# Gathering, turning and modulating all context rows once, in the router, instead of per expert

## The reference, cut to what matters

```
h    = modulate(rms_norm(y, norm_ffn), shift, scale)   # shift, scale differ for latent and context
aff  = softmax over tokens of (h @ w_router)           # 16 experts
g, idx = top_k(aff, cap)                               # each expert: 128 latent, 32 context tokens
xs   = h[idx]
ys   = (silu(xs @ w_gate) * (xs @ w_up)) @ w_down * g
y    = y + gate * scatter_add(ys, idx)
y_out = rms_norm(y, norm_final)
```

## Time and profile before

| what | us |
|---|---|
| median of 3 runs | 4124.34 (4119.36 to 4125.55) |
| span of the profiled execution | 4118.9 |
| PE / PEld / DVE / ACT / POOL busy | 3849.3 / 3382.8 / 2463.8 / 1832.2 / 503.2 |
| mean granted clock of PE, as a share of full speed | 0.968 |

### The profile page before, as it was taken

One profiled execution on the slowest core, in us unless ns is written; L12 is line 12 of the kernel. 1 busy time (PEld: TensorE's weight loads), 2 busy tenths in 40 slices (PEclk: granted clock), 3 DMA queues, 4 the chain that ended last, 5 costly groups with the idle time before them and its releaser, 6 DMA issues. The chain is left out here.

```text
span 4118.9 us, 68560 instructions
## 1 busy us (share of the span) xinstructions
PE 3849.3 (93%) x25046; PEld 3382.8 (82%) x25046; DVE 2463.8 (60%) x4732; ACT 1832.2 (44%) x2910; POOL 503.2 (12%) x501
## 2 busy tenths in 40 slices
PE   7899999999799999799997799999999999999992
PEld 3688888888688888799996688888888888888881
DVE  4645555555366666322325677777777777777774
ACT  3611111111267776211104566666666666666653
POOL 0000000000264653000000000000000000000000
PEclk9999999999899999899998799999999999999996
DMA  9434444444465553736316577778777777788876
GB/s 348 154 128 133 133 129 133 136 132 127 142 177 162 180 181 117 256 113 222 113 54 252 173 255 258 252 252 264 253 251 251 252 256 253 255 264 261 259 238 247
DMA packets 572379, 825.46 MB, mean 200 GB/s; under 512 B 23728, under 2 KB 458368, under 8 KB 560512
## 3 DMA queue, kind: packets, MB, share of 16 engines
q1 hardware_dynamic: 548448, 700.96, 52.1%
q0 software_dynamic: 23840, 123.26, 9.4%
HBM read 717.21 MB, written 108.00 MB: 200 GB/s over the span
## 5 line engine op out<-in xcount | busy, mean ns | idle before, releaser
L1977 DVE TENSOR_TENSOR e_wlo<-e_raw,e_whi 128x1024 fp32r<-128x1024 f32 x768 | 905.0, 1219 | 346.1 <-ACT e_whi L1897 342.9
L2109 PE MATMUL ps<-e_xs,e_whi 128*128 128x320 f32 x4096 | 1061.1, 345 | 13.9 <-DVE e_xs L1985 7.8
L2109 PE MATMUL ps<-e_xs,e_wlo 128*128 128x160 f32 x4096 | 935.3, 239 | 0.0
L1897 ACT ACTIVATE e_whi<-e_raw 128x1024 fp32r<-128x1024 f32 x768 | 768.6, 1054 | 321.2 <-DMA e_raw<-in_w_down 107.7
L2109 PEld LDWEIGHTS ps<-e_xs,e_whi 128*128 128x128 f32 x4096 | 755.2, 188 | 22.3 <-DVE e_wlo L1977 10.6
L2109 PEld LDWEIGHTS ps<-e_xs,e_wlo 128*128 128x128 f32 x4096 | 771.7, 191 | 0.7
L2127 PE MATMUL ps<-e_whi,e_h 128*128 128x512 f32 x1024 | 405.6, 396 | 8.5 <-DVE e_h L2011 8.5
L488 PE MATMUL ps<-hhi,p_whi 128*128 128x512 f32 (+1 forms) x1536 | 386.6, 360 | 8.5 <-DVE p_wlo L427 8.5
L445 DVE SCALAR_TENSOR_TENSOR p_acc<-p_modraw,cT,p_acc 128x256 f32<-128x256 f32 x960 | 386.4, 477 | 0.5 <-DMA p_modraw<-in_w_mod 0.5
L488 PE MATMUL ps<-hlo,p_whi 128*128 128x512 f32 (+1 forms) x1536 | 383.4, 358 | 0.0
L488 PE MATMUL ps<-hhi,p_wlo 128*128 128x512 f32 (+1 forms) x1536 | 383.1, 358 | 0.0
(11 more groups left out here) (245 smaller groups left out, 5498.7 us busy)
## 6 DMA issues: line engine op xcount, KB each, us to landing
e_raw<-in_w_gate SPq DMA_DIRECT2D x64, 2048.0 KB
e_raw<-in_w_up SPq DMA_DIRECT2D x64, 2048.0 KB
e_raw<-in_w_down SPq DMA_DIRECT2D x64, 2048.0 KB
p_modraw<-in_w_mod SPq DMA_DIRECT2D x128, 512.0 KB, 3.6
m_raw<-in_w_mod SPq DMA_DIRECT2D x16, 2048.0 KB, 14.6
p_raw<-in_w_in SPq DMA_DIRECT2D x64, 512.0 KB, 4.7
o_raw<-in_w_out SPq DMA_DIRECT2D x16, 2048.0 KB, 8.6
projT<-p_out_st POOLq DMA_DIRECT2D x32, 640.0 KB, 3.4
```

Of the source, the lines that this page charges most:

```text
L1897: nc.scalar.activation(piece(whi, c, q), piece(raw, c, q), ACT.Copy).then_inc(w_hi_made, 1)
L1977: nc.vector.tensor_tensor(piece(wlo, c, q), piece(raw, c, q), piece(whi, c, q).bitcast(F32), ALU.subtract).then_inc(w_lo_made, 1)
L2109: last = nc.tensor.matmul(bank[:, 0:cols], w[:, s, at:at + P], xs[:, k, 0:cols], start=(k == 0 and w is whi), stop=(k == KD - 1 and w is whi))
```

## The change

The context rows of all experts (16 x 32 = 512 rows) are gathered in four indirect DMAs of 128 rows (`idxG`, one column for each), into the first four tiles of `yt`, as soon as the fourth round of choosing is over. To have the 512 indices as four columns of 128, DVE spreads the 16 x 32 table by group (`numS`) and PE makes one small product with `group_of`. PE turns the four tiles (64 turns), ACT scales and shifts them (16 instructions of 512 columns) into a new tile `ctxT`, 128 x 16 x 512. The tables `gC` and `idxC` are turned and copied at the same place. In the instruction list of PE all this stands ahead of the turn of the latent tables.

In `experts`, POOL gathers only 128 latent rows, PE turns only these, in 4 groups of 4 blocks (two groups after each of the first two down chunks), ACT modulates only latent columns, and the context columns of `xs` are filled from `ctxT` by one ACT instruction (`ctx_high`) and one DVE instruction (`ctx_lo`) per expert, after the groups. To make room for `ctxT`, buffers are shared: gathered rows and `ys_l` are one tile `rows_l`, so `scale_ys` waits for the turns of the column blocks that it overwrites; `gact`, `hf` and `ctx_sum` go, their results written in place.

```diff
 # router, POOL
             pool.wait_ge(xn_stored, 16 * NT)
+            pool.wait_ge(ctx_step, 6)
+            for g in range(NCG):
+                nc.gpsimd.indirect_dma_start(yt[:, g, :], None, xn_d, bass.IndirectOffsetOnAxis(idxG[:, g:g + 1], 0)
+                                             ).then_inc(ctx_gathered, 16)
+            pool.wait_ge(ctx_gathered, 16 * NCG)
 # router, ACT
+            for k in range(KD):
+                act.wait_ge(ctx_turned, k + 1)
+                nc.scalar.activation(ctxT[:, k, :], ps[:, k % 4, :], ACT.Identity, bias=addT[:, 1, k:k + 1],
+                                     scale=mulT[:, 1, k:k + 1]).then_inc(ctx_modulated, 1)
 # router, PE
+            pe.wait_ge(ctx_step, 3)
+            for n, src in enumerate((topC, numC)):
+                nc.tensor.transpose(ps[0:CAP_C, 5, n * E:n * E + E], src[:], ident[0:E, 0:E]).then_inc(slots_turned, 1)
+            pe.wait_ge(ctx_step, 4)
+            nc.tensor.matmul(ps[:, 6, 0:NCG], numS[:].rearrange("e a s -> e (a s)"), group_of[:], start=True, stop=True
+                             ).then_inc(ctx_step, 1)
+            pe.wait_ge(ctx_gathered, 16 * NCG)
+            for k in range(KD):
+                if k < 4:
+                    pe.wait_ge(gate_read, 4 + k + 1)
+                else:
+                    pe.wait_ge(ctx_modulated, k - 3)
+                for g in range(NCG):
+                    last = nc.tensor.transpose(ps[:, k % 4, g * P:g * P + P], yt[:, g, k * P:k * P + P], ident[:])
+                last.then_inc(ctx_turned, 1)
+            for n, src in enumerate((topL, numL)):
+                pe.wait_ge(pick_step, PICKS + 7)
+                nc.tensor.transpose(ps[0:CAP_L, 7, n * E:n * E + E], src[:], ident[0:E, 0:E]).then_inc(slots_turned, 1)
 # router, DVE, in the rounds of choosing
+                if r == CAP_C // 8 - 1:
+                    nc.vector.tensor_copy(topC[:], top[64:64 + E, 0:CAP_C]).then_inc(ctx_step, 1)
+                    nc.vector.tensor_copy(numC[:], place[64:64 + E, 0:CAP_C]).then_inc(ctx_step, 1)
+                    ...
+                elif r == CAP_C // 8:
+                    dve.wait_ge(ctx_step, 5)
+                    nc.vector.tensor_copy(idxG[:], ps[:, 6, 0:NCG]).then_inc(ctx_step, 1)
+                    dve.wait_ge(slots_turned, 2)
+                    slots(CAP_C, 5, v["gC"], v["idxC"])
 # experts, ACT
+            def ctx_high(n):
+                act.wait_ge(xs_turned, n * NGR + NGR)
+                nc.scalar.activation(xs[:, :, CAP_L:CAP], ctxT[:, :, ds(n * CAP_C, CAP_C)], ACT.Copy).then_inc(xs_hi, 1)
 # experts, DVE
+            def ctx_lo(n):
+                dve.wait_ge(xs_hi, n * XSTEPS + XSTEPS)
+                nc.vector.tensor_tensor(xs[:, :, CAP + CAP_L:2 * CAP], ctxT[:, :, ds(n * CAP_C, CAP_C)],
+                                        xs[:, :, CAP_L:CAP].bitcast(F32), ALU.subtract).then_inc(xs_made, 1)
...
+                if not last:
+                    dve.wait_ge(xs_turned, e * NGR + (NGR + d + 1))
-                nc.vector.scalar_tensor_tensor(out=ys_l[:, cols], in0=ps[:, bank, :], scalar=aff_l[:, 0:1],
+                nc.vector.scalar_tensor_tensor(out=rows_l[:, cols], in0=ps[:, bank, :], scalar=aff_l[:, 0:1],
 # experts, PE, turn_xs
-                    for k in range(k0, k1):
-                        at = (k - k0) * CAP
-                        nc.tensor.transpose(ps[:, r % XB, at:at + CAP_L], xg_l[:, k * P:k * P + P], ident[:])
-                    for k in range(k0, k1):
-                        at = (k - k0) * CAP
-                        last = nc.tensor.transpose(ps[:, r % XB, at + CAP_L:at + CAP], xg_c[:, k * P:k * P + P],
-                                                   ident[0:CAP_C, 0:CAP_C])
+                    for i in range(KG):
+                        k = r * KG + i
+                        last = nc.tensor.transpose(ps[:, r, i * CAP_L:i * CAP_L + CAP_L], rows_l[:, k * P:k * P + P],
+                                                   ident[:])
```

More of the change, by code:

```diff
@@ L1547, in _ @@
                 act.wait_ge(y_turned, 4 * t + 4)
[L1548 removed]
+                nc.scalar.activation(yt[:, t, :], yt[:, t, :], ACT.Copy, scale=rinv[:, t:t + 1]).then_inc(y_scaled, 1)
             for c in range(2):
@@ new lines, in _ @@
+            dve.wait_ge(pick_step, PICKS)
+            nc.vector.tensor_copy(num[:], place[:]).then_inc(pick_step, 1)
+            nc.vector.tensor_copy(topB[:], top[32:32 + E, ::-1]).then_inc(pick_step, 1)
+            dve.wait_ge(pick_step, PICKS + 2)
+            nc.vector.tensor_scalar(numB[:], num[32:32 + E, ::-1], float(HALF), None, ALU.add).then_inc(pick_step, 1)
+            nc.vector.tensor_tensor(first[:], top[0:E, :], topB[:], ALU.is_ge).then_inc(pick_step, 1)
+            nc.vector.tensor_tensor(topL[:], top[0:E, :], topB[:], ALU.max)
@@ new lines, in _ @@
+            dve.wait_ge(pick_step, PICKS + 4)
+            nc.vector.tensor_tensor(numL[:], num[0:E, :], numB[:], ALU.subtract).then_inc(pick_step, 1)
+            dve.wait_ge(pick_step, PICKS + 5)
+            nc.vector.tensor_tensor(numL[:], numL[:], first[:], ALU.mult).then_inc(pick_step, 1)
+            dve.wait_ge(pick_step, PICKS + 6)
+            nc.vector.tensor_tensor(numL[:], numL[:], numB[:], ALU.add).then_inc(pick_step, 1)
+            dve.wait_ge(slots_turned, 4)
+            slots(CAP_L, 7, v["gL"], v["idxL"])
@@ L1765, in experts @@
     SLOTS = 2 * NP
-    NGR = 6
-    XB = 4
-    TURNS = (range(0, XB), range(XB, NGR))
-    GROUPS = [(3 * r, min(3 * r + 3, KD)) for r in range(NGR)]
+    NGR = 4
+    KG = KD // NGR
+    TURNS = (range(0, 2), range(2, NGR))
+    XSTEPS = NGR + 1
     index_set = sem("e_index_set")
@@ L1775, in experts @@
     xs_made = sem("e_xs_made")
-    gate_row, raw, w_loaded = (v[n] for n in ("gate_row", "raw", "w_loaded"))
+    gate_row, raw, w_loaded, ctxT = (v[n] for n in ("gate_row", "raw", "w_loaded", "ctxT"))
     w_hi_made = sem("e_w_hi_made")
@@ L1958, in expert @@
                         xs_high(e + 1, TURNS[c - NUP - 1])
+                        if c == NUP + 2:
+                            ctx_high(e + 1)
                 copy_ctx_low(e, ND - 1)
@@ L1964, in _ @@
                 xs_high(0, groups)
+            ctx_high(0)
             with act.Fori(0, E - 1) as e:
@@ L2049, in expert @@
                     else:
-                        scale_ys(e, c - NUP - 1)
+                        scale_ys(e, c - NUP - 1, last)
                     if following:
@@ L2061, in expert @@
                         build_xs(e + 1, TURNS[c - NUP - 1])
-                scale_ys(e, ND - 1)
+                        if c == NUP + 2:
+                            ctx_lo(e + 1)
+                scale_ys(e, ND - 1, last)
             make_lo(0, 0, range(NP))
             build_xs(0, range(NGR))
+            ctx_lo(0)
             with dve.Fori(0, E - 1) as e:
```

145 lines of the change are left out of this document (63 added, 82 removed).

## The result

The changed kernel takes 4055.31 us, median of 4 runs (4046.81 to 4061.72), against 4122.81 for the kernel before on the same chip: ratio 0.9835, 95% interval 0.9821 to 0.9849. That is 67.5 us less, where 27.5 were forecast: the right sign, but outside the range. The profiled execution has a span of 4055.2, 63.7 less than 4118.9; the rest of the 67.5 is scatter of the runs.

A forecast was written before the change was run, and what follows sets the result against it. The prediction took PE's own work to bound the expert loop. Its terms, -31.5 loop, +10.5 router, -1.8 and -4.7 first expert, summed to -27.5 us, giving 4096.8 us, range 4082 to 4114.

The forecast's parts named there:

- So weights come late for ACT without coming late for PE: Expert loop: PE sat idle only 13.9 us ahead of 4096 products while ACT waited 321 us, so PE's work sets the end.
- up to 1 us per expert: Expert loop, low end of the range only: PE's present idle time of up to this size could go too.
- What comes in its place runs on ACT and DVE: Expert loop: context copies replace PE's context turns, ACT gets some 4.7 us less per expert, and slack covers them.
- 16 latent turns at 2.1 us: PE's turns per expert: 4.19 us falls to 2.1, saving 2.1 each, 15 times, -31.5 us.
- least that goes: PE's turns per expert: the 16 context turns at 0.10 us, about 1.6 us, are the smallest saving.
- The gathers: 18.5 us: Router: four context gathers of 4.19 MB take 4.2 us fixed plus the bytes at 293 GB/s, landing at 2269.1.
- The 64 turns at half clock: 17.9 us: Router: PE's context turns at 0.28 us each, with the clock at 0.50 throughout, done at 2287.0.
- The rival's 13.3: Router: clock rises after about 8 us of the 64 turns; rival with this or faster gathers: 4092, chance 0.22.
- +10.5 for the router: Router: gathers, 64 turns and latent tables make it end at 2287.8 instead of 2277.3.
- The first expert's -6.5: Ahead of the first expert's products: gather 1.8 us shorter, first turn to first product 4.7 us shorter.
- The rival in which weights become the bound: Expert loop: weight loads bind and the loop gives nothing, leaving the router's +4.0 alone, 4128; chance 0.10.
- The slow rival: Expert loop: strided context copies take 13.8 us instead of 1.3 and hold up first products, +121, 4218; chance 0.05.

The follow-up runs named there:

- e10: Kernel before with one 160-column ACT modulation per block (context columns wrong) and context rows gathered for the first expert only; 0.9914 of the kernel before.
- e3: Kernel before, each block modulated by one ACT instruction of 160 columns with latent constants, so context columns are wrong; 0.9995 of the kernel before.
- e4: Kernel before, context rows gathered for the first expert only and used by all others, so outputs are wrong; 0.9952 of the kernel before.
- e2: Kernel before with the same PE turns sorted, all latent blocks of a call first, then all context blocks; 1.0003 of the kernel before, 4128.42 us.
- e7: Changed kernel with each latent modulation cut into two ACT instructions of 96 and 32 columns; 0.9924 of the kernel before, 4094.24 us.
- e8: Changed kernel with POOL's gather for the next expert held until about 40 us into the expert instead of 14; 0.9844 of the kernel before, 4056.92 us.
- e11: Changed kernel with DVE modulating every second group of four latent blocks instead of ACT; 0.9832 of the kernel before.
- e5: Changed kernel run again unedited, on another chip; 0.9834 of the kernel before, 4050.91 us.
- e6: Changed kernel with POOL also gathering the next expert's 32 context rows in the loop, unused; 0.9878 of the kernel before, 4072.53 us.
- e1: Changed kernel with 16 unused turns of 32 rows per expert put back on PE after the first down chunk; 0.9894 of the kernel before, 4083.01 us.

## Why the prediction was wrong

Shorter turns in a loop that PE bounds, paid for with a gather and 64 turns in the router, were the right terms, though each had the wrong size. One mechanism was missing: ACT's lighter load and the smaller gather shorten waits of PE that the prediction took for absent. Of the 35.8 us between the forecast 27.5 and the 63.3 found below, 17.5 are that, 7.8 the turns, 9.3 the router and the first expert, 1.3 the last expert.

- **The bound in the loop: the step that failed.** "So weights come late for ACT without coming late for PE" was read from PE's idle column; the rows of its weight loads, above, show 27 us of waits for low parts (10.6 + 16.2). PE's products took 1.7 us per expert more than their least, 0.9 in the gate and up part and 0.8 in the first down chunk. The change removed 1.1 of it; with smaller pieces that is 17.5 us in the loop, for which the sum had nothing, and only the low end of the range had "up to 1 us per expert". That end was also added up wrongly: 38 and 15 from 4124.3 is 4071, not 4082, and 4055 lies below both. e10 shows the cause by doing it alone, with PE's turns kept: less work for ACT alone gives nothing (e3), the smaller gather alone 20 us (e4), both 35.
- **"What comes in its place runs on ACT and DVE", 4.7 us less for ACT, priced at nothing.** ACT's busy time fell by 4.3 us per expert (68.8 to 64.5). The 6.5 us of slack that I read for `xs` in the earlier trace rows were not the tight place. e2 showed one: context results of the second down chunk, behind the modulations on ACT. With ACT's load of before, the shorter turns are worth little: e7 (0.9924), which has them, is 12 us faster than e4 (0.9952), which does not, instead of the 39 of the turns (over two chips, with intervals of 8 us either way).
- **16 latent turns at 2.1 us.** They take 1.6. The turns of the earlier trace rows start 0.109 us apart, just as those in the loop; its 1.97 us hold the tail, which overlaps the next row, and I rounded up from there. Fifteen experts give 39, not 31.5. The "least that goes", 0.10 per context turn, left out what each going to and fro between the two heights costs, and that is what e2 took away.
- **The gathers: 18.5 us.** They took 13.6, near the 14.0 of the lower bound: 6.1 for the first and 2.5 for each of the other three, 1.05 MB in 2.5 us or 420 GB/s, near the 426 of plain loads. The rate of 293 GB/s that I took held a fixed time already. The Trainium skill's formula for a software DMA (DMA: Bandwidth & Descriptors, Anatomy of one DMA) had given 11.6 as an estimate; this trace is between the two forecasts.
- **The 64 turns at half clock: 17.9 us.** They took 10.7. The clock rose 4.4 us into them, and the rows above show that only turns ran. The rival's 13.3 was nearer. The rule of the Trainium skill that transposes do not count as a busy PE (TensorE: Matmul & The Clock Gate, Part 4: PE-mode transpose) does not hold in this trace, which decides; I had let it stand beside a stretch of 7 us that was too short to tell.
- **+10.5 for the router** was +1.1, since DVE's rounds, and not the turns, ended last: near the floor of 1.6 that I had worked out. **The first expert's -6.5**: its first product comes 19.4 us behind the last table instead of 25.8, -6.4, as forecast (10.55 us from the first turn to the first product, 10.3 forecast). Together -5.3 instead of +4.0.

The sum again, with measured sizes: 39.3 of turns, 17.5 of waits and small pieces, 1.3 in the last expert, 5.3 between the first round and the first product, 63.3 in all. The first round starts 0.7 later, and what follows the last product is 1.1 shorter, which makes the 63.7. The rival in which weights become the bound was wrong in its sign: weights were in part a bound already, and the change loosened it. The slow rival fell: `ctx_high` and `ctx_lo` take about 0.7 us each.

Why does removing a wait in the gate and up part (e8, e11) bring 0.5 us back in the first down chunk, while in many experts of the changed kernel neither has one? The traces tell where. The load of the second down chunk waits until DVE has made the low part of the last up chunk, so its issue marks how late DVE runs. In e5, e8, e11 and the changed kernel, where the gate and up part has no wait and that load goes out by 61.6 us after the first product, the first down chunk takes 9.2 us; from 61.9 on it takes 9.3 to 10.3, and what ends the wait is `e_h`, made by DVE. In e8 the moved gather makes it late. In e11 it is late from the third chunk on, with DVE's eight modulations as the likely cause; no run separates that.

What stays open: why the fourth chunk's load takes 9 us in one expert and 13.5 in another, with additions, gather and loads issued at nearly the same places.

## What to carry to other kernels

Idle time ahead of PE's products understates waits: look at its weight loads too, compare the same stretch over its repetitions, and ask why the mean is above the least. When two engines are nearly level, the price of removing work from one is nothing (e2), and from the other nothing (e3), and from both it is more than the sum; so check for each engine at which instruction the other waits for it last. A small software gather is not priced by its bytes but by the load that it delays.

## What the runs showed of the hardware

- 0.25 MB more of gathered rows per expert cost 21.6 us in 15 experts (e6). Every fifth chunk's load took 11.4 us or more instead of 9.8 or more, and three loads of the fourth chunk took 14.7 to 15.3, where the changed kernel's slowest takes 13.5 (14.0 in e5).
- At clock 1.00, turns of 128 rows start 0.109 us apart in any run (router, before, e2, changed), 32-row turns 0.062 (e1, e2). A change from 128 to 32 rows takes 0.20 instead of 0.109, one back 0.15 instead of 0.062 and 0.165 for the next turn (before, e2).
- The granted clock rose from 0.50 to 1.00 with nothing but transposes on PE, 4.4 us after they began and after 15 us of idle; the seven other traces with these 64 turns show the same, 3.7 to 4.7 us after the start.
- At clock 0.50 the turns of a run start 0.213 us apart (16 take 3.68 us with the tail); the 0.28 of the earlier trace rows was again the mixture.
- A 1 MB gather alone landed after 6.8 us; of four in flight the first took 6.1 and the others 2.5 each.
